# Reordering both ends of a hybrid decoder step: first token block in two column parts, last two norms interleaved

## What is computed

```python
def rms_norm(x, g):
    xf = x.astype(jnp.float32)
    y = xf * lax.rsqrt(jnp.mean(xf * xf, axis=-1, keepdims=True) + RMS_EPS)
    return (y * g.astype(jnp.float32)).astype(x.dtype)

h = rms_norm(x, attn_norm)
z = jnp.einsum('btd,de->bte', h, w_in)        # q_a, ckv, krope, u, qm, gate
...
mix = jnp.concatenate([mla_out, pool_out, cross_out], axis=-1) * jax.nn.silu(gate)
x = x + jnp.einsum('bte,ed->btd', mix, w_out)
y = rms_norm(x, final_norm)
```

## Time and profile before

| | us |
|---|---|
| median of 3 runs | 869.02 |
| lowest, highest | 868.46, 870.1 |
| the profiled execution | 869.34 |
| its span, first to last instruction | 866.7 |
| TensorE matmul busy | 855.5 (99% of the span) |
| TensorE weight load busy | 780.0 (90%) |
| VectorE busy | 591.4 (68%) |
| ScalarE busy | 464.2 (54%) |
| GpSimd busy | 146.3 (17%) |
| mean DMA rate | 194 GB/s |

### The profile page before, as it was taken

How to read it: one execution, slowest core, us unless ns; L and a number is a source line. 1 busy time by engine, 2 the same in 40 slices (tenths; PEclk the granted TensorE clock), 3 DMA queues, 4 the chain that set the end, 5 groups by cost and what they waited for, 6 DMA issues and landing times.

```text
span 866.7 us, 15863 instructions
## 1 busy us (share of the span) xinstructions
PE 855.5 (99%) x5549; PEld 780.0 (90%) x5549; DVE 591.4 (68%) x1021; ACT 464.2 (54%) x774; POOL 146.3 (17%) x210
## 2 busy tenths in 40 slices
PE   8999999999999999999999999999999999999996
PEld 8999999999989999999999999888887788888885
DVE  6546635532358688888888875966678889564777
ACT  6565422122233566676667654577777546363445
POOL 0003001411300112323232330000000112111123
PEclk9999999999999999999999999999999999999998
DMA  9695435222365587878888754524137685979576
GB/s 356 252 338 187 160 131 179 78 83 102 102 256 184 175 274 245 258 251 249 253 255 249 248 165 143 212 85 158 37 110 302 148 223 113 261 203 275 112 147 218
DMA packets 64878, 168.56 MB, mean 194 GB/s; under 512 B 9672, under 2 KB 27657, under 8 KB 62808
## 3 DMA queue, kind: packets, MB, share of 16 engines
q1 hardware_dynamic: 52528, 126.48, 42.6%
q0 software_dynamic: 10752, 33.56, 17.0%
q10 hardware_dynamic: 1520, 7.51, 2.4%
HBM read 156.14 MB, written 11.50 MB: 193 GB/s over the span
## 4 chain that ended last, share of the span: by engine, by line
PE 96%; DVE 2%; ACT 1%; issue 1%; DMA 0%; ACTq 0%; DVEq 0%
PE z L67 8%; PE z L69 8%; PE z L68 8%; PE z_acc L67 6%; PE z_acc L68 6%; PE z_acc L69 6%; PE pa_s L67 4%; PE pa_s L69 4%; PE pa_s L68 4%; PE kv_acc L67 3%; PE pa_qk L69 3%; PE pa_qk L68 3%; PE pa_qk L67 3%; PE kv_acc L68 3%; PE kv_acc L69 3%; PE ps_s L1428 2%
## 5 line engine op out<-in xcount | busy, mean ns | idle before, releaser
L67 PE MATMUL z<-x_hi,w_hi 128*128 128x288 f32 x512 | 152.5, 298 | 0.0
L69 PE MATMUL z<-x_hi,w_lo 128*128 128x288 f32 x512 | 150.8, 294 | 0.0
L68 PE MATMUL z<-x_lo,w_hi 128*128 128x288 f32 x512 | 150.7, 294 | 0.0
L184 ACT ACTIVATE w_hi<-w_raw 128x1024 fp32r<-128x1024 f32 (+2 forms) x62 | 64.8, 1045 | 138.6 <-PE z L69 54.9
L191 DVE TENSOR_TENSOR w_lo<-w_raw,w_hi 128x1024 fp32r<-128x1024 f32 (+2 forms) x62 | 77.5, 1250 | 70.2 <-ACT w_hi L184 69.8
L1021 POOL DMA_DIRECT2D v_raw<-in_cache x128 | 69.3, 541 | 176.0 <-issue 173.6
L67 PEld LDWEIGHTS z<-x_hi,w_hi 128*128 128x128 f32 x512 | 96.1, 188 | 2.7 <-issue 1.1
L68 PEld LDWEIGHTS z<-x_lo,w_hi 128*128 128x128 f32 x512 | 96.1, 188 | 1.6 <-issue 0.2
L69 PEld LDWEIGHTS z<-x_hi,w_lo 128*128 128x128 f32 x512 | 96.0, 188 | 0.0
L2049 ACT ACTIVATE o_hi<-o_raw 128x1024 fp32r<-128x1024 f32 x50 | 52.9, 1060 | 70.4 <-PE pa_s L3017 38.4
L2297 DVE TENSOR_TENSOR o_lo<-o_raw,o_hi 128x1024 fp32r<-128x1024 f32 x50 | 60.9, 1220 | 35.0 <-ACT o_hi L2049 34.8
(11 more groups left out here) (553 smaller groups left out, 2403.4 us busy)
## 6 DMA issues: line engine op xcount, KB each, us to landing
w_raw<-in_w_feat SPq DMA_DIRECT2D x56, 512.0 KB, 3.7
k_raw<-in_cache SPq DMA_DIRECT2D x128, 192.0 KB, 3.1
v_raw<-in_cache POOLq DMA_DIRECT2D x128, 128.0 KB, 3.3
o_raw<-in_w_out POOLq DMA_DIRECT2D x30, 512.0 KB, 8.1
o_raw<-in_w_out SPq DMA_DIRECT2D x20, 512.0 KB, 8.3
w_raw<-in_w_mem_kv SPq DMA_DIRECT2D x16, 512.0 KB, 3.6
gate_spill<-gate_tmp SPq DMA_DIRECT2D x16, 288.0 KB, 3.6
mix<-gate_spill SPq DMA_DIRECT2D x4, 1152.0 KB, 9.6
```

What stands on the lines that cost most here:

```text
L67: pe.matmul(out, a[0], b[0], start=start, stop=False, skip_group_check=onto)
L68: pe.matmul(out, a[0], b[1], start=False, stop=False, skip_group_check=onto)
L69: return pe.matmul(out, a[1], b[0], start=False, stop=stop, skip_group_check=onto)
L184: act.activation(hi_slot(s, u)[:, lo:w], s.wraw[:, u % RAW, lo:w], ACT.Copy).then_inc(s.w_hi, 1)
```

## The change

Front: SyncE loads token block 0 in two parts (columns 0 to 255, then 256 to 575, with a semaphore of its own), then the rest of unit 0, then chunk 2. Block 1 goes to ScalarE's queue as its third transfer. There the piece of unit 0 comes first, the norm's vector second. ScalarE's split of the rest of unit 0 now stands ahead of its wait for block 1. State and tables are issued after round 2's weights, the pool weight after round 3's.

End: VectorE adds block 3's first half before it works out block 2's norm; block 3's columns 1536 to 2047 are no longer multiplied by the gain ahead of time (one operation multiplies by both factors later); the statistics are kept at a quarter, the root is then half of it, and with m the quarter of the mean square plus epsilon and h the half root, the factor is 1 / (h + m / h), in three links (reciprocal, multiply-add, reciprocal) instead of four; ScalarE squares block 3's first half before it scales block 2; SyncE stores block 2's columns 1024 to 1535 instead of ScalarE.

```diff
@@ SyncE, front
-            x_chunk(0)
+            sp.dma_start(xraw[:, 0, 0:FIRST_X], a["xT"][:, 0, 0:FIRST_X]).then_inc(xt_landed[0], 16)
+            sp.dma_start(xraw[:, 0, FIRST_X:T], a["xT"][:, 0, FIRST_X:T]).then_inc(x0_rest, 16)
             sp.dma_start(s.wraw[:, 0, KV:unit_width(0)], a["w_kv"][0][:, KV:unit_width(0)]).then_inc(s.w_landed[0], 16)
-            x_chunk(1)
             x_chunk(2)
...
-                if i == 1:
+                if i == 2:
                     sp.dma_start(s0[:, 0:GR * DB * STATE], a["state_t"]).then_inc(st_in, 16)
...
-                if i == 2:
+                if i == 3:
                     sp.dma_start(wpr[:], a["w_pool_t"]).then_inc(wp_in, 16)
@@ ScalarE, front
+            act.dma_start(s.wraw[:, 0, 0:KV], a["w_kv"][0][:, 0:KV]).then_inc(w0_in, 16)
             act.dma_start(gx[:], a["attn_norm_c"]).then_inc(gx0_in, 16)
-            act.dma_start(s.wraw[:, 0, 0:KV], a["w_kv"][0][:, 0:KV]).then_inc(w0_in, 16)
+            k0, k1 = X_CHUNKS[1]
+            act.dma_start(xraw[:, k0:k1, :], a["xT"][:, k0:k1, :]).then_inc(xt_landed[1], 16)
...
             for c, (k0, k1) in enumerate(X_CHUNKS):
+                if c == 1:
+                    split_hi(act, s, 0, 1, KV)
                 act.wait_ge(xt_landed[c], 16)
                 for k in range(k0, k1):
-                    if k == 1:
-                        split_hi(act, s, 0, 1, KV)
-                    elif k and k % KV_K == 0:
+                    if k > 1 and k % KV_K == 0:
                         split_hi(act, s, k // KV_K, k // KV_K + 1)
                     if k < 2:
                         act.activation(xhi[:, k, 0:FIRST_X], xraw[:, k, 0:FIRST_X], ACT.Identity, scale=gx[:, k:k + 1]).then_inc(x0_hi, 1)
+                        if k == 0:
+                            act.wait_ge(x0_rest, 16)
@@ SyncE, end
+                if n == 0:
+                    sp.wait_ge(y_right, 8)
+                    sp.dma_start(rows[:, 1024:1536], tile_block(i, 0, 1)).then_inc(out, 16)
@@ ScalarE, end: the new order
+            act.wait_ge(added, 16)
+            square(tile_block(2, 1, 0), 2, 3)
+            act.wait_ge(squared, 19)
+            act.wait_ge(y_rest, 2)
+            half_root(0, 3)
+            act.wait_ge(added, 17)
+            square(v3[:, 0:256], 3, 3)
+            scale_right(0)
+            act.wait_ge(added, 18)
+            square(v3[:, 256:512], 3, 9)
+            act.wait_ge(squared, 21)
+            act.wait_ge(y_rest, 3)
+            half_root(1, 9)
+            scale_right(1)
+            act.wait_ge(y_right, 10)
+            act.dma_start(a["o_y_p"][3 * P:4 * P, 1024:1536], tile_block(3, 0, 1)).then_inc(out, 16)
@@ VectorE, end: the norm, and the new order
+            def quarter_mean(n, last):
+
+                y_link(dve.scalar_tensor_tensor(out=yt.st[:, 6, cols[n]], in0=last, scalar=0.25 / D, in1=yt.st[:, 4, cols[n]], op0=ALU.mult, op1=ALU.add))
                 dve.wait_ge(root, 2 + n)
-                y_link(dve.reciprocal(r, root_))
-                y_link(dve.scalar_tensor_tensor(out=t_, in0=r, scalar=r, in1=yt.st[:, 6, col], op0=ALU.mult, op1=ALU.mult))
-                y_link(dve.tensor_scalar(t_, t_, -0.5, 1.5, ALU.mult, ALU.add))
-                dve.tensor_tensor(r, r, t_, ALU.mult).then_inc(y_inv, 1)
+                half = yt.st[:, 5, cols[n]]
+                y_link(dve.reciprocal(yt.st[:, 8, cols[n]], half))
+                y_link(dve.scalar_tensor_tensor(out=yt.st[:, 8, cols[n]], in0=yt.st[:, 6, cols[n]], scalar=yt.st[:, 8, cols[n]], in1=half,
+                                                op0=ALU.mult, op1=ALU.add))
+                dve.reciprocal(yt.st[:, 7, cols[n]], yt.st[:, 8, cols[n]]).then_inc(y_inv, 1)
...
+            dve.tensor_scalar(yt.st[:, 4, 3:5], yt.st[:, 6, 3:5], 0.25 / D, 0.25 * EPS, ALU.mult, ALU.add).then_inc(y_rest, 1)
+            dve.wait_ge(tile_done, 2)
+            dve.tensor_tensor(v3[:, halves[0]], v3[:, halves[0]], ybank[:, 1, halves[0]], ALU.add).then_inc(added, 1)
+            dve.wait_ge(squared, 19)
+            dve.wait_ge(y_rest, 2)
+            quarter_mean(0, yt.st[:, 3, cols[0]])
+            scale_left(0)
+            dve.wait_ge(squared, 20)
+            dve.scalar_tensor_tensor(out=yt.st[:, 4, cols[1]], in0=yt.st[:, 3, cols[1]], scalar=0.25 / D, in1=yt.st[:, 4, cols[1]],
+                                     op0=ALU.mult, op1=ALU.add).then_inc(y_rest, 1)
+            dve.wait_ge(added, 17)
+            dve.tensor_tensor(yt.yo[1][:, halves[0]], v3[:, halves[0]], gl[:, halves[0]], ALU.mult).then_inc(y_last, 1)
+            dve.wait_ge(tile_done, 3)
+            dve.tensor_tensor(v3[:, halves[1]], v3[:, halves[1]], zbank[:, 1, halves[1]], ALU.add).then_inc(added, 1)
+            dve.wait_ge(added, 18)
+            dve.tensor_tensor(yt.yo[1][:, halves[1]], v3[:, halves[1]], gl[:, halves[1]], ALU.mult).then_inc(y_last, 1)
+            dve.wait_ge(squared, 21)
+            dve.wait_ge(y_rest, 3)
+            quarter_mean(1, yt.st[:, 9, cols[1]])
+            scale_left(1)
```

More of the change, by code:

```diff
@@ L2266, in _, with half_root, scale_right @@
             squares(1, 1, 1, 2)
-            for n, i in enumerate((2, 3)):
-                col = slice(COL[i], COL[i] + 1)
-                last = tile_block(i, 1, 0)
-                if i == 2:
-                    act.wait_ge(added, 16)
-                    square(last, i, 3)
-                    act.wait_ge(squared, 19)
-                    act.wait_ge(y_rest, 2)
-                else:
-                    for c in range(2):
-                        act.wait_ge(added, 17 + c)
-                        square(last[:, 256 * c:256 * c + 256], i, 9 if c else 3)
-                    act.wait_ge(squared, 21)
-                    act.wait_ge(y_rest, 3)
-                act.activation(yt.st[:, 5, col], yt.st[:, 9 if i == 3 else 3, col], ACT.Sqrt,
-                               bias=yt.st[:, 4, col], scale=1.0 / D).then_inc(root, 1)
+            v3 = tile_block(3, 1, 0)
+            def half_root(n, row):
+                col = slice(COL[2 + n], COL[2 + n] + 1)
+                act.activation(yt.st[:, 5, col], yt.st[:, row, col], ACT.Sqrt, bias=yt.st[:, 4, col], scale=0.25 / D).then_inc(root, 1)
+            def scale_right(n):
                 act.wait_ge(y_inv, 2 + n)
                 for l in range(2):
-                    v = tile_block(i, 0, l)
-                    act.activation(v, v, ACT.Copy, scale=yt.st[:, 7, col]).then_inc(y_right, 1)
-                act.wait_ge(y_right, 6 + 2 * n + 2)
-                act.dma_start(a["o_y_p"][P * i:P * i + P, 1024:1536], tile_block(i, 0, 1)).then_inc(out, 16)
+                    v = tile_block(2 + n, 0, l)
+                    act.activation(v, v, ACT.Copy, scale=yt.st[:, 7, COL[2 + n]:COL[2 + n] + 1]).then_inc(y_right, 1)
+            act.wait_ge(added, 16)
[14 more added lines that the diff above has]
+            act.dma_start(a["o_y_p"][3 * P:4 * P, 1024:1536], tile_block(3, 0, 1)).then_inc(out, 16)
             act.wait_ge(root, 3)
@@ new lines, in _ @@
+            cols, halves = [slice(COL[i], COL[i] + 1) for i in (2, 3)], [slice(256 * c, 256 * c + 256) for c in range(2)]
+            v2, v3 = tile_block(2, 1, 0), tile_block(3, 1, 0)
+            def quarter_mean(n, last):
+                y_link(dve.scalar_tensor_tensor(out=yt.st[:, 6, cols[n]], in0=last, scalar=0.25 / D, in1=yt.st[:, 4, cols[n]], op0=ALU.mult, op1=ALU.add))
+                dve.wait_ge(root, 2 + n)
+                half = yt.st[:, 5, cols[n]]
[3 more added lines that the diff above has]
+                dve.reciprocal(yt.st[:, 7, cols[n]], yt.st[:, 8, cols[n]]).then_inc(y_inv, 1)
+                dve.wait_ge(y_inv, 2 + n)
@@ new lines, in scale_left @@
+            def scale_left(n):
+                w, r = tile_block(2 + n, 1, 1), yt.st[:, 7, cols[n]]
+                dve.scalar_tensor_tensor(out=w, in0=w, scalar=r, in1=gr, op0=ALU.mult, op1=ALU.mult).then_inc(yscaled, 1)
+                dve.wait_ge(y_last, 1 if n == 0 else 3)
+                dve.tensor_scalar(yt.yo[n], yt.yo[n], r, None, ALU.mult).then_inc(yscaled, 1)
+            dve.wait_ge(tile_done, 1)
+            dve.wait_ge(added, 8 + ADDED[Q7])
+            dve.tensor_tensor(v2, v2, ybank[:, 0, :], ALU.add).then_inc(added, 1)
@@ new lines, in _ @@
+            dve.wait_ge(added, 16)
+            dve.tensor_tensor(yt.yo[0], v2, gl, ALU.mult).then_inc(y_last, 1)
+            dve.wait_ge(squared, 18)
+            y_link(dve.reduce_sum(yt.st[:, 6, 3:5], yt.st[:, 0:3, 3:5].rearrange("p r c -> p c r"), AX))
+            dve.tensor_scalar(yt.st[:, 4, 3:5], yt.st[:, 6, 3:5], 0.25 / D, 0.25 * EPS, ALU.mult, ALU.add).then_inc(y_rest, 1)
+            dve.wait_ge(tile_done, 2)
+            dve.tensor_tensor(v3[:, halves[0]], v3[:, halves[0]], ybank[:, 1, halves[0]], ALU.add).then_inc(added, 1)
```

43 lines of the change are left out of this document (1 added, 42 removed).

## The result

The changed kernel took 870.38 us in the median of 22 runs (869.03 to 873.34), the kernel before 868.88 us in as many beside it: ratio 1.0016, 95% interval 1.001 to 1.0023. That is slower by 0.16%, 1.5 us, where 1.06 us less was forecast, and it is outside the range. The profiled execution took 871.30 us with a span of 868.2 us, 1.5 us more than before, so its trace holds the whole loss.

The account below looks back on a forecast made before the run. TensorE was taken to bound the kernel, holding 96% of the path that sets the end. Front -0.26, tables 0 and end -0.8 us summed to -1.06 us: median 868.0 us, range 867.0 to 869.2 us.

Parts of the forecast that it names:

- The first matmul: Opening: first real matmul, at 6.87 us, comes 0.45 us earlier because ScalarE's weight piece is issued one place earlier.
- the cap of 0.26 us: Opening: TensorE gains at most 0.26 us, since block 2 can't be read before 10.26 us if chunk 2's landing is unchanged.
- The bytes in front of chunk 2 on both queues together are the same, so I leave its landing where it is.: Opening: chunk 2 lands as before, at about 8.45 us, 6.2 us after issue.
- The front term: Opening: the edits to the first loads change the time by -0.26 us.
- My bound of 0 to -0.70 us: Opening: no gain if chunk 2 comes 0.26 us later, -0.70 us if it comes earlier.
- I take no cost for it: Opening: the norm's vector, issued 0.45 us later on ScalarE's queue, costs nothing, being needed only after ScalarE's weight copy.
- Rival A: Opening: chunk 2 lands earlier with block 1 off its queue; front -0.7 us, total 867.4 us; chance 0.15.
- Rival B: Opening: block 0's shorter packets make chunk 2 0.26 us or more later; 868.2 us, or 868.4 us; chance 0.12.
- The tables: State and tables issued one round later, near 58 us: 0 us, state landing at 68.1 us with 3.6 us of cover.
- Rival D: Moved tables: state arrives too late and holds TensorE up; 871.3 us if landing 17 us after issue; chance 0.05.
- The end: Last stretch: VectorE's last addition 1.05 us and block 3's first store 1.0 us earlier; bytes limit the gain to 0.8 us.
- Rival C: End: no gain, stores being serial in bytes with block 2's queued on SyncE; only the front stays, 868.8 us; chance 0.10.

Follow-up runs that it names:

- c2: The changed kernel, unchanged, profiled again on the same chip as the second profile of the kernel before; no ratio, block 1 read at 10.52 us, block 4 at 17.19 us.
- c1: The kernel before, unchanged, profiled again as a control; no ratio, block 1 read at 8.55 us, block 4 at 15.21 us.
- h2: Second run of the kernel before with only block 1 moved to third on ScalarE's queue; ratio 1.0029 (1.0018 to 1.0041).
- g1: The kernel before with block 1 third on ScalarE's queue and chunk 2 held back until block 1 landed; no ratio, block 1 landed at 5.9 us.
- e9: The kernel before with ScalarE's first two transfers exchanged, weight piece ahead of the norm's vector; ratio 0.9996 (0.9984 to 1.0008).
- e2: The kernel before with only block 1 moved to third on ScalarE's queue; 871.06 against 868.75 us, ratio 1.0023.
- h1: The kernel before with block 1 third on ScalarE's queue and ScalarE splitting the rest of unit 0 before waiting for it; ratio 1.0011 (1.0003 to 1.002).
- e8: The kernel before with only token block 0 loaded in two column parts; ratio 1.0005 (0.9995 to 1.0015).
- e4: The kernel before with only state, tables and pool weight issued one round later; 868.89 against 868.75 us, ratio 1.0.
- e3: The kernel before with only the new end; 868.05 us, ratio 0.9993 (0.9984 to 1.0003).
- g4: The kernel before, unchanged, profiled as a control on another chip; no ratio, block 1 read at 8.66 us, block 4 at 15.31 us.

## Why the prediction was wrong, point by point

**The first matmul.** 0.45 us earlier was forecast and measured (6.42 us). It was worth nothing, not even the cap of 0.26 us. It could have come earlier still: in after the row of low halves begins at 4.95 us and holds two in 1.00 us, so the first is done at about 5.45 us, which by my 0.12 us makes 5.57 us. In after and in c2 (6.09 us) the warm-up on ones was in the way:

```profile
1.28 5.49 PE L725 MATMUL z_acc<-ones 128*128 128x128 f32 x24 [1.28 <-POOL ones L359]
```

These 24 rows took 4.34 us in the kernel before, 5.29 us in c1 and 5.05 us in c2.

**"The bytes in front of chunk 2 on both queues together are the same, so I leave its landing where it is."** This is the step that failed, in two ways. Chunk 2 did not land when it did, it came 1.2 us later (7.4 us for 6.2). And above all it was the only transfer that I asked about. I called it "what is late next", and took the rest of unit 0 and block 1 for as punctual as before, though one had a new neighbour and the other a new queue. They decided: 8.2 us for 5.1 and 9.0 us for 5.9. The front term was +1.71 us instead of -0.26 us. Equal bytes say something of when a stretch is all through, nothing of which transfer in it is complete first: in one queue the needed ones go first, in two they share, and the slowest engine's last packets take turns with the other's (h2; not so in g1). My bound of 0 to -0.70 us came from chunk 2 alone and so could not hold it. "I take no cost for it" held for `gx` in after with nothing to spare (its last count came at 4.38 us, ScalarE read it at 4.41 us), and was wrong where block 0 is whole: 0.43 us of waiting in e9, more than the slack.

The Trainium skill, page "DMA: Bandwidth & Descriptors", section "Issuing engines are not separate DMA queues", was right in its direction: chunk 2 gained nothing by the second queue in after. Rival A's earlier landing showed once (7.2 us in e2; 8.4 and 8.7 us in h1 and h2, and 7.7 to 8.7 us in the six traces of the old opening), its gain never, since TensorE waited for block 1 first. That the transfers interleave is what h2's rows show. I drew from it that the sum stays, and did not ask who loses by interleaving. The same page of the Trainium skill, section "Queues, rings and completion order", goes further: each DMA engine takes turns between the queues that it has work for, a packet of several descriptors at a time. That speaks against this change, since block 1 then shares the engines with chunk 2 instead of going ahead of it. The trace agrees on the turns: 65 packets of block 1 beside 60 in h2 from 5.5 to 6.5 us, and one for one on the last engine from 8.38 to 9.79 us. It differs on their size: a turn there is one row of 2304 or 3840 bytes, not several.

**Rival B** had the right suspect in part (e8: chunk 2 at 9.3 us, wait before block 2). At block 4 it was worth 0.7 us (0.8 against c1) rather than 0.2, and it is not the mechanism that cost most by itself; together with block 1's move it is what made unit 0 late.

**The tables.** Term 0, right (e4: ratio 1.0). The state landed in 5.4 us rather than 10.2. The copies came at 65.1 us, so "no room to speak of" was in truth 5 us. Rival D did not come near.

**The end.** The engines' part was right within 0.1 us: first store of block 3 1.07 us nearer to TensorE's end, 1.0 forecast, with VectorE's last addition 0.32 us behind the last matmul's start (0.43 forecast). The bytes gave 0.61 us in after and 0.66 us in e3's slices, where I had 0.7 to 0.9. The stretch ran as steadily as assumed, but it began at 861.7 us with 1.31 MB to move instead of 1.28, in a kernel that was 0.09 us later. Over all nine traces with the new end the tail is 7.99 to 8.28 us, over the eleven with the old one 8.61 to 8.68 us. Rival C is dead.

**The range.** Its upper end was the front at no gain plus scatter. No rival put a loss in the opening of more than 0.2 us, so 0.07 for slower was all on a mechanism in another place.

## What to carry to other kernels

Where two queues feed the same stretch, price every transfer that is needed early, not only the one that is late today: to move one of them to a second queue costs it its place in line, and here it landed 2 to 4 us later with the same bytes around it. A transfer is as late as the slowest of its 16 engines, so one execution's landing says little about the next. Keep the transfers of an opening on one queue in the order of need. An engine that works in program order should do the work whose data came first before it waits for the next; here that was worth about 1 us when a landing was late.

## What the runs showed of the hardware

**Two queues take turns row by row on each DMA engine, and a transfer waits for its slowest engine.** In h2, 11 packets took from 7.5 to 10.1 us beside 178 of the other queue (83 + 44 + 51), and from 8.06 us on they were one engine's; alone on the wire (g1) the whole transfer of 288 KB landed after 4.1 us.

**After 3.7 us without a matmul h2's TensorE worked at the lower clock.** So long had it been idle when block 1 came. The windows at 10, 12 and 17 us (columns as above):

```profile
10.00:11.00 1.00, 0.00 (x0) 0.00 (x0) 0.07 (x1) 0.84 (x2) 0.00 (x0) 1.00 0.89 370
...
12.00:13.00 1.00, 0.70 (x3) 0.73 (x4) 1.00 (x3) 0.97 (x3) 0.00 (x0) 0.50 1.08 445
...
17.00:18.00 1.00, 1.00 (x5) 1.00 (x5) 0.96 (x3) 1.00 (x2) 0.00 (x0) 0.50 0.99 415
```

The granted clock fell from 1.00 to 0.50 (1.2 GHz) and stayed there to about 18 us (0.98 from 18 to 19 us). TensorE got from block 1 to block 4 in 9.25 us instead of 6.66 us (c1). That is how a landing 1.8 us later than e2's became 4.4 us at block 4. After's idle time of 1.6 us and c2's of 2.4 us left the clock at 1.00. The 6.2 us (21.55 against 15.31 us in g4) were there in full at the last matmul (864.24 against 857.99 us). Whether after's longest runs (up to 873.34 us) are such executions is not shown, since none of them was profiled. For it speaks that its four longest spans (869.2 to 870.5 us) came with a granted clock of 0.995 or 0.996, all the others with 0.997 or 0.998.

**Less rate where block 0 comes in two parts.** With block 0 in two parts and block 1 on the second queue the engines moved 268 and 305 GB/s in the two windows above, at a busy share of 0.86 and 0.97; the six traces of the old opening have 310 to 353 and 340 to 404 GB/s (the earlier trace rows is one), e8, with the split alone, 308 and 311, and e2, block 1 moved but no split, 417 and 443 GB/s. The records of the single packets say a little more. From 4 to 8 us 45 of after's 402 packets took over 1.5 times as long as is usual for their size (one of 4608 bytes 1.47 us instead of 0.18), 23 of 527 in before, none of 607 in e2. Why they do stays open.
